# A hybrid RWKV and conformer layer: the prompt unit's steps, the conv layer norm and the head norms in one mixed sequence, w_out with the prompt tile last, router weights side by side

## What is computed

```python
h = rms_norm(x) * (1 + sc1) + sh1
z = h @ w_in                                # 2816 columns
y_rwkv = bidirectional RWKV-7 scan of z     # 8 heads x 64, chunks of 64 tokens
y_rwkv = layer_norm per head (y_rwkv) * (sigmoid(z_g) @ gate_lora_b)
y_conv = silu(layer_norm over 512 channels (depthwise conv of width 31))
x = x + g1 * (concat(y_rwkv, y_conv) @ w_out)
h = rms_norm(x) * (1 + sc2) + sh2
logits = h @ router_group_w (4 columns), h @ router_expert_w (32 columns)
x = x + g2 * top-2 of 8 experts in the top-1 of 4 groups
outputs: rms_norm(x) of prompt and sample tokens, final states of the prompt scan
```

## Time and profile before

| | us |
|---|---|
| median of 3 runs | 1273.71 |
| the profiled execution's own time | 1268.37 |
| its span in the trace | 1266.5 |
| TensorE busy in the span | 949.6 (75%) |
| VectorE busy | 610.0 (48%) |
| ScalarE busy | 293.9 (23%) |
| GpSimd busy | 63.3 (5%) |

### The profile page before, as it was taken

How to read it: one execution, slowest core, us unless ns; L and a number is a source line. 1 busy time by engine, 2 the same in 40 slices (tenths; PEclk the granted TensorE clock), 3 DMA queues, 4 the chain that set the end, 5 groups by cost and what they waited for, 6 DMA issues and landing times. The chain is left out here.

```text
span 1266.5 us, 15551 instructions
## 1 busy us (share of the span) xinstructions
PE 949.6 (75%) x5991; PEld 598.4 (47%) x5991; DVE 610.0 (48%) x1283; ACT 293.9 (23%) x499; POOL 63.3 (5%) x55
## 2 busy tenths in 40 slices
PE   1699988989488778786867666997359998589654
PEld 1365555666275565774756533554333433134221
DVE  2317999364667678678772342424631111011106
ACT  2240000321615335166021243101001111011002
POOL 0000000000010010010100000000111111010000
PEclk9999997999566575575665867987559999799878
DMA  9845512101100110011005191111189999799633
GB/s 326 301 183 203 210 44 71 60 18 26 17 10 18 18 26 17 2 27 17 10 24 163 49 366 78 50 50 50 57 313 375 420 419 419 319 401 420 278 123 140
DMA packets 72745, 193.77 MB, mean 153 GB/s; under 512 B 42310, under 2 KB 42816, under 8 KB 58464
## 3 DMA queue, kind: packets, MB, share of 16 engines
q1 hardware_dynamic: 64416, 174.19, 36.7%
q0 software_dynamic: 5472, 10.53, 2.3%
q10 hardware_dynamic: 2783, 8.06, 1.7%
HBM read 181.80 MB, written 19.34 MB: 159 GB/s over the span
## 5 line engine op out<-in xcount | busy, mean ns | idle before, releaser
L544 PE MATMUL bank<-arena 128*128 128x320 f32 x704 | 201.3, 446 | 12.2 <-DVE arena L436 3.8
L544 PEld LDWEIGHTS bank<-arena 128*128 128x128 f32 x704 | 136.1, 196 | 79.0 <-issue 28.0
L2031 PE MATMUL bank<-arena 128*64 128x512 f32 (+2 forms) x528 | 130.7, 655 | 33.6 <-DMA arena<-in_expert_w_up 32.6
L944 DVE SCALAR_TENSOR_TENSOR arena<-arena 128x655 f32<-128x655 f32 x116 | 104.7, 902 | 4.6 <-DVE arena L944 0.2
L2031 PEld LDWEIGHTS bank<-arena 128*64 128x64 f32 (+2 forms) x528 | 46.1, 149 | 116.4 <-issue 115.0
L1475 PE MATMUL bank<-arena 128*128 128x512 f32 x160 | 76.9, 643 | 11.6 <-issue 11.6
L2111 DVE TENSOR_TENSOR arena<-arena,bank 128x256 f32<-128x256 f32 x17 | 7.2, 422 | 159.8 <-ACT arena L2085 159.8
L2053 PE MATMUL bank<-arena 128*64 128x512 f32 (+2 forms) x264 | 62.4, 599 | 9.9 <-DVE arena L2114 9.9
L906 ACT ACTIVATE arena<-bank 64x128 f32<-64x128 f32 (+1 forms) x68 | 19.9, 292 | 174.3 <-PE bank L1279 173.0
L1475 PEld LDWEIGHTS bank<-arena 128*128 128x128 f32 x160 | 32.8, 208 | 53.0 <-issue 53.0
L1270 PE MATMUL bank<-arena 64*64 64x64 f32 x320 | 25.6, 302 | 40.9 <-DVE arena L1129 33.2
(11 more groups left out here) (321 smaller groups left out, 1445.8 us busy)
## 6 DMA issues: line engine op xcount, KB each, us to landing
arena<-in_expert_w_gate SPq DMA_DIRECT2D x33, 1024.0 KB, 17.0
arena<-in_expert_w_up SPq DMA_DIRECT2D x33, 1024.0 KB, 20.4
arena<-in_expert_w_down SPq DMA_DIRECT2D x33, 1024.0 KB, 18.8
arena<-in_ada_w SPq DMA_DIRECT2D x12, 2048.0 KB, 10.6
arena<-in_w_in SPq DMA_DIRECT2D x22, 512.0 KB, 3.7
arena<-expert_rows SPq DMA_DIRECT2D x10, 512.0 KB, 7.3
arena<-in_x_sample SPq DMA_DIRECT2D x8, 512.0 KB, 7.5
arena<-in_w_out SPq DMA_DIRECT2D x1, 4096.0 KB, 15.9
```

Source lines behind the costliest of these rows:

```text
L544: mm = nc.tensor.matmul(psum[4 + 2 * (n % 2) + half][:, 0:HALF], wring[:, n % NWIN, k], hT[:, k, half * HALF:(half + 1) * HALF], start=(k ...
L944: chain(nc.vector.scalar_tensor_tensor(acc, src, w, acc, ALU.mult, ALU.add))
L2031: mm = nc.tensor.matmul(psum[2 + n % 2][r, :], xeT[:, n % 2, c, r], gu[:, :, c, :], start=(c == 0), stop=(c == KD - 1))
```

## The change

The chain events of unit 4 leave the lists of `order()` and are called one by one from `pe_out`, `dve_out` and `act_out`, with work of the stage behind between them. The convolution's loads move into SyncE's `final`, behind the load of `w_out` and waits for the reads of the PSUM banks of unit 4. The head norms are split into sample tokens (one piece of 512 columns for each pair) and prompt tokens (all four pairs as one piece of 512 columns). The squares and deviations have buffers of their own. w_out takes the tiles 1, 2, 3, 4, 0. The two router matrices are loaded side by side into one array of 36 columns. The sums of the tiles are announced in halves. GpSimd's clearing waits for the last turned tile instead of the logits. In the cut diff the places left out are, in order: two rows of `g1b`; `sh2b`, `gain2` and `norm2_g`; the eight stores of the states; then `late`, the router's weights and biases, `g2b` and the two fixed experts; on TensorE the 8 products each for conv's sums and squares, and behind the gates the prompt heads' mean and four gates of 128 columns, whose variance comes after the first half of tile 1; on VectorE conv's centring (8 instructions), its variance, and at the end conv's scaling (4), the four sample pairs' scaling and gating (8), then the prompt's; on ScalarE four squares of conv, and at the end Ln of four pairs, Exp of conv and of four pairs, four Silu, and the prompt's square, Ln and Exp.

```diff
@@ order() @@
-                       for u in range(NU) for i in range(steps(u)) for ev in CHAIN]
+                       for u in range(NU - 1) for i in range(steps(u)) for ev in CHAIN]
@@ sp_mix(), event final @@
                     sp.dma_start(wout, ins["w_out"][0].rearrange("(k p) n -> p k n", p=P)).then_inc(s_wout, 16)
-                    sp.wait_ge(s_finc, 1)
-                    for a in range(8):
-                        sp.dma_start(outs["new_state"][0, 0, a // 4, 2 * (a % 4):2 * (a % 4) + 2]
...
+                    for use in ("z0", "z1", "y0", "y1", "b0", "b1", "v0", "v1", "v2", "v3", "m0", "m1", "m2", "m3"):
+                        wait_read(sp, u, use)
+                    for stored in s_cst:
+                        sp.wait_ge(stored, 32)
+                    for j in range(4):
+                        sp.dma_start(conv[:, j], cout[j]).then_inc(s_conv_in, 16)
@@ sp_out() @@
+            sp.wait_ge(s_gvar, 5)
+            for i in (1, 2, 3, 0):
+                sp.dma_start(x2[:, i], tok_src(i)).then_inc(s_x2in, 16)
             sp.wait_ge(s_Y, step_at(NU - 1, 2))
...
+            sp.wait_ge(s_cn, 4)
+            sp.dma_start(x2[:, 4], tok_src(4)).then_inc(s_x2in, 16)
...
+            sp.wait_ge(s_finc, 1)
...
+            sp.wait_ge(s_finst, 128)
+            sp.wait_ge(s_mixa, PAIRS)
...
@@ pe_out() @@
+            pe_mix([("X", LAST, 0)])
+            y_mean(0)
+            y_mean(1)
+            pe_mix([("T", LAST, 0)])
...
             pe.wait_ge(s_conv_in, 64)
...
+            pe_mix([("S", LAST, 0), ("Y", LAST, 0)])
+            pe.wait_ge(s_gsq, 4)
...
+            pe_mix([("X", LAST, 1)])
+            y_var(0)
+            y_var(1)
+            pe_mix([("T", LAST, 1)])
+            y_mean(2)
+            y_mean(3)
+            pe_mix([("S", LAST, 1), ("Y", LAST, 1)])
+            y_gate(0)
+            y_gate(1)
+            y_var(2)
+            y_var(3)
+            pe_mix([("final", LAST, 0)])
+            y_gate(2)
+            y_gate(3)
...
             pe.wait_ge(s_mixa, 4)
             pe.wait_ge(s_mixc, 4)
             pe.wait_ge(s_wout, 16)
...
+                for k in range(KD):
+                    mm = nc.tensor.matmul(psum[6][:, 36 * i:36 * i + 36], h2T[:, k], rw_[:, k],
+                                          start=(k == 0), stop=(k == KD - 1))
...
+            for q, i in enumerate(WTILES):
                 if i == 0:
+                    pe.wait_ge(s_mixa, 5)
...
@@ dve_out() @@
+            dve_mix(chain, [("X", LAST, 0)])
+            y_centre(0, 1)
+            y_centre(1, 2)
+            dve_mix(chain, [("T", LAST, 0)])
...
+            dve_mix(chain, [("S", LAST, 0), ("Y", LAST, 0)])
...
+            dve_mix(chain, [("X", LAST, 1)])
+            y_variance(0)
+            y_variance(1)
+            dve_mix(chain, [("T", LAST, 1)])
+            y_centre(2, 4)
+            y_centre(3, 5)
+            dve_mix(chain, [("S", LAST, 1), ("Y", LAST, 1)])
+            y_variance(2)
+            y_variance(3)
...
@@ act_out() @@
+            act_mix(chain, [("T", LAST, 0)])
...
             square(0)
+            square(1)
+            act_mix(chain, [("T", LAST, 1)])
+            square(2)
+            square(3)
+            act_mix(chain, [("final", LAST, 0)])
+            act.wait_ge(s_gv, 1)
+            chain(nc.scalar.activation(rstd, rstd, ACT.Ln))
...
@@ pool_route() @@
-            pool.wait_ge(s_wo, TILES)
-            pool.wait_ge(s_lg, TILES)
+            pool.wait_ge(s_wo, 2 * TILES)
+            pool.wait_ge(s_h2t, TILES)
```

More of the change, by code:

```diff
@@ L740, in sp_mix @@
             sp = nc.sync
-            for ev, u, i in order("sp"):
+            for ev, u, i in order("sp") + [("final", NU - 1, 0)]:
                 if ev == "w":
@@ L923, in gc @@
                 return x.rearrange("p (g c) -> p g c", c=C)
-            chain(nc.vector.memset(VP[:, 0:C], 0.0))
-            chain.announce(nc.vector.memset(E1[:, :, 0:1], 1.0), s_pads, 1)
-            for ev, u, i in order("dve"):
+            for ev, u, i in events:
                 if ev == "z":
@@ L1158, in pool_mix, with pe_mix @@
                                                            ALU.mult), s_bkh, u + 1)
-        def pe_mix():
+        def pe_mix(events):
             pe = nc.tensor
-            for ev, u, i in order("pe"):
+            for ev, u, i in events:
                 if ev in ("z", "ada", "join"):
@@ L1335, in build @@
         xtmp, xsq, sq_pos = regs.take(D), regs.take(D), regs.take(D)
[L1336 removed]
+        rw_, rb = regs.take(KD, 36), regs.take(36)
         h2T = view(zbase + 3 * PAIRS * ZT + ZT, KD, P)
[L1338 removed]
+        routing = Region(ebuf[NB - 1], ebuf[NB - 1] + ROUTING)
         h2d = dram("tokens_for_experts", [T, D])
@@ L1432, in pe_out @@
+            for use in ("z0", "z1"):
+                wait_read(pe, LAST, use)
             pe.wait_ge(s_conv_in, 64)
@@ L1532, in dve_out @@
             for j in range(4):
                 chain.announce(nc.vector.tensor_tensor(conv[:, j], conv[:, j], rstd, ALU.mult), s_cn, j + 1)
-            dve.wait_ge(s_modb, 16 * 8)
-            for c in range(2):
-                chain(nc.vector.scalar_tensor_tensor(gain2[:, c], gain2[:, c], 1.0, h2, ALU.add, ALU.mult))
-            dve.wait_ge(s_x2in, 16 * TILES)
-            def taken(i):
-                dve.wait_ge(s_h2t, i + 1)
+            for j in range(PAIRS):
+                y = ysum[:, j, TP:T]
+                g, b_ = PAR["gng"] + j, PAR["gnb"] + j
+                dve.wait_ge(s_gstd, j + 2)
+                chain(nc.vector.scalar_tensor_tensor(y, y, par[:, g:g + 1], rstd_y[:, j], ALU.mult, ALU.mult))
+                dve.wait_ge(s_gate, j + 1)
+                chain.announce(nc.vector.scalar_tensor_tensor(y, y, par[:, b_:b_ + 1], psum[j % 2][:, :],
+                                                              ALU.add, ALU.mult), s_mixa, j + 1)
@@ new lines, in dve_out @@
+            dve.wait_ge(s_gstd, 6)
+            for j in range(PAIRS):
+                g = PAR["gng"] + j
+                chain(nc.vector.scalar_tensor_tensor(yp[:, j], yp[:, j], par[:, g:g + 1], rstd_p[:, j],
+                                                     ALU.mult, ALU.mult))
+            dve.wait_ge(s_gate, 5)
+            for j in range(PAIRS):
+                b_ = PAR["gnb"] + j
+                ins_ = nc.vector.scalar_tensor_tensor(yp[:, j], yp[:, j], par[:, b_:b_ + 1],
+                                                      psum[7][:, j * P:(j + 1) * P], ALU.add, ALU.mult)
+                if j < PAIRS - 1:
+                    chain(ins_)
@@ L1543, in taken @@
+            chain.announce(ins_, s_mixa, 5)
+            dve.wait_ge(s_x2in, 16 * (TILES + 2))
+            def taken(q):
+                dve.wait_ge(s_h2t, q + 1)
                 chain.announce(nc.vector.tensor_copy(h2T[:, 4:8], psum[5][:, :].rearrange("p (k t) -> p k t", t=P)),
-                             s_h2Td, i + 1)
-            for i in range(TILES):
+                             s_h2Td, q + 1)
+            for q, i in enumerate(WTILES):
                 c = int(i > 0)
-                dve.wait_ge(s_wo, i + 1)
@@ L2200, in _ @@
             chain = act_front()
-            act_mix(chain)
+            act_mix(chain, order("act"))
             act_out(chain)
@@ L2211, in _ @@
             chain = dve_front()
-            dve_mix(chain)
+            dve_pads(chain)
+            dve_mix(chain, order("dve"))
             dve_out(chain)
@@ L2230, in _ @@
             pe_front()
-            pe_mix()
+            pe_mix(order("pe"))
             pe_out()
```

302 lines of the change are left out of this document (149 added, 153 removed).

## The result

The changed kernel takes 1224.13 us (median of 4 runs, 1220.1 to 1225.81), the kernel before 1273.75 (4 runs beside them): a ratio of 0.961, 95% interval 0.9584 to 0.9636. That is 49.6 us less; forecast were 40.6. The profiled execution took 1223.6 with a span of 1221.9, so against the span before (1266.5) the traces account for 44.6 us. As far as these traces show, much of the spread between executions lies ahead of the change: in the eleven profiles with the change (its first, its repeat and nine with one or two edits), the prompt unit's chain starts between 687.5 and 694.0. So the stages are compared by their lengths, each from a first instruction to the next stage's first: the zeroed state on VectorE (L1107 before, L1110 after), the first w_out product, the first routing instruction (128x180), the end.

The account below looks back on a forecast made before the run. No engine bounds the kernel throughout; 88 us ahead of w_out are handing over between engines. Parts A -26.0, B -11.6 and C -3.0 sum to -40.6 us: 1233.1 against the median 1273.7, range 1224 to 1254.

Parts of the forecast that it names:

- Part A: Merged stage ahead of w_out: norm and conv work laid into the prompt chain's gaps, w_out starting about 750.5, -26.0 us.
- the wait: TensorE ahead of w_out's first turn, waiting for h2 and its positions: stall of 0 to 5.5 us, taken as +1.5.
- the chain as it was: 27.2 us: First term of part A: the prompt unit's chain along TensorE, from 688.3 to 715.5, at its old duration.
- the walk: Part A's count along TensorE, then ScalarE and VectorE, to w_out: -26.0 us; -32.5 at full clock, -7.5 at 1.2 GHz.
- The conv loads and the fixed experts' loads: Moved loads: conv's land at 694, wanted at 698; the fixed experts' go out near 764, used after routing; both covered.
- Part B: w_out: variance +0.9, logits -6.3 and -3.5, last tile -4.2, first turn's stall +1.5, together -11.6 us.
- The rule on turn-taking: Positions' DMA beside the fixed experts' loads: engines alternate queues by packet, so landing about 6 us, stall 1.
- Part C: GpSimd's clearing ends before the logits, so VectorE's second routing instruction takes about 0.2 instead of 3.22 us: -3.0.
- 1 (half clock throughout): Merged stage: clock stays at 1.2 GHz, part A only -7.5, in all -22, 1251.6 us; chance 0.15.
- 2 (late positions): First w_out turn: positions land after 10.6 us, TensorE stalls 5.5, in all -36.6, 1237.1 us; chance 0.12.
- 3, 4 and 5: Table switches cost 2.6 us more (0.03); conv loads 26 us late, 1259.1 (0.02); w_out at 1.2 GHz, 1299.4 (0.03).
- three signs of being wrong: PEclk 0.50 from 697 to 735, TensorE idle before the first turn waiting for h2, or a longer expert stage.

Follow-up runs that it names:

- experiment 6: The changed kernel with Ln and Exp alternating again for conv and the four sample pairs, ten table loads instead of two: 1234.59 us.
- experiments 4 and 8: The changed kernel with the first positions' DMA issued earlier: 1218.22 us; with SyncE issuing the fixed experts' loads only after those positions landed: 1217.16 us.
- experiment 3: The changed kernel with GpSimd's clearing of the gather buffers behind the last logits again: 1227.32 us.
- experiment 5: The changed kernel with w_out's tiles in the order 0, 1, 2, 3, 4 again, the prompt first: 1232.8 us.
- experiment 7: The changed kernel with five products of 512 columns that nobody reads put on TensorE ahead of the first turn: 1223.81 us.

## Why the prediction was right, point by point

- **Direction and range**: held, the range by luck: the median is 1224.13 with the end at 1224, and two of the four runs (1223.6 and 1220.1) lie below it. Each mechanism of parts A to C was seen; two sizes were off, part A's by 6 us and the wait's by 5.5.
- **Part A, -26.0; measured -32.0.** The term that was mis-sized is the first, "the chain as it was: 27.2 us". I priced what was added at its clock, and left the chain's own products at their durations of before. In the trace the copies of the end states begin at 725.1 and end at 726.3, 38.8 us after the chain's start, not 43.1 behind it. T is 1.3 shorter and the first S and Y take 3.2 us where they took 5.0; over both steps the chain's own products are together some 5 us shorter. The transposes of the end states take 1.04, at full clock, where I had added 1, and the gates and variances ahead of them 3.5 instead of 4.5. The squares, on the other side, were late by 2.14, which I had counted as nothing. With the events put back ahead of the norms (experiment 1) T is at 3.67 again. From the copies to w_out 17.4 us (19.0 in the walk). That is close to my lower bound, the walk at full clock (-32.5).
- **The table loads**: 1.28 each and no more, shown by experiment 6.
- **The conv loads and the fixed experts' loads**: the first were covered, as said. The second were covered as to their own use, but not as to what they hold up. They went out at 752.6 to 755.7, just ahead of the positions at 756.4.
- **Part B, -11.6; measured -10.1, near by errors of opposite sign.** Laid side by side, the rows of the two kernels give: the four logits blocks on the path -10.1 at equal clock, against -9.8; the tiles behind them -2.0, which I had at nothing; the first two tiles -1.8, since w_out now starts at full clock; the variance +0.9 and the tail -4.1, as counted (the last turn waits 5.52 us behind VectorE, with no positions); the wait +4.4, and turn and logits at half clock behind it +2.6, where I had +1.5 for both. Experiment 2, which puts the 32 records back, finds more for the logits, 13.8 to 15.6; experiments 4 and 8 find 7.0 to 8.8 for the wait. The wait's mechanism was named, with its bound (landing after 10.6, a stall of 5.5); the value I chose between the ends was the wrong one, with 8.8 measured where I took 6.5. The positions were issued 1.3 us earlier than I had them and TensorE wanted h2 2.0 earlier. And the price of the wait left out that the clock falls in it.
- **The rule on turn-taking** (the Trainium skill, DMA: Bandwidth & Descriptors, Queues, rings and completion order) had given, as an estimate, about 6 us for the landing; the trace shows 8.8, between it and the gathers' 10.6. The trace agrees that the transfer does not wait behind all 6 MB: it landed at 765.2, while the last of the six loads, issued before it at 755.7, took 19.2 us.
- **Part C, -3.0**: 3.22 to 0.18 in the row; in the stage 2.2 us against the first profile of the change and 3.7 against the repeat (experiment 3). My argument that a PSUM operand isn't held rested on a row whose instruction started 0.05 us before the clearing; it came to no test.
- **Rivals**: 1 (half clock throughout) is refuted by 1.00 in 697 to 715.6; 2 (late positions) came true in mechanism and price (4.4 for the wait alone, 5.5 forecast), hidden in the total by the larger gains; 3, 4 and 5 did not happen. TensorE idle in front of the first turn was one of the three signs of being wrong, and it was seen; the first w_out record at 743.7 was just ahead of the 744 to 757 named as right; the rest (370.5 and 369.0 against 372 less 3) and the table loads came as said.
- **Total**: against the profiled execution's own time I forecast 1227.8 and it was 1223.6. The remaining 5 us between 44.6 and 49.6 fit the profiled execution of before, a short one (5.4 below its median); where in the span it was short no trace shows.

What stays open: how the 19.6 us of the regrouping divide. Experiment 6 puts the table loads at 6.5 to 8.1 us in the new order, and experiment 5 the prompt's heads ahead of w_out at 8.9 to 10.5. Each was taken back alone, never both together; that they add up to the 19.6 is not shown, and fewer hand-overs, the moved loads and split columns were only argued. Open too is why one tile in four behind a full-clock logits block takes 15.68 us and not 13.98.

## What to carry to other kernels

Work laid into the gaps of a latency-bound chain can pay twice: here the gaps were used, and TensorE's clock stayed up for the chain's own products as well (1.00 against 0.80). Price the whole stretch at the clock it will have, not only the additions. When a bulk load moves, ask what small transfer it now meets: a half-MB load with 6 MB beside it took 8.8 us instead of 3.7, and one wait or an earlier issue gave back more than most of the planned terms. Short products whose records cost the same whatever their columns are worth merging, here for more than their own time (11.7 us in the blocks, 13.8 to 15.6 in the stage). And repeat the profile of the unchanged version before you give a microsecond of a stage to a cause.

## What was not expected of the hardware

- A wait of 4.39 us on TensorE cost 7.0 to 8.8: by the rows the wait itself, turn 1.97 instead of 1.04 and logits 3.60 instead of 1.95. Filling the wait with products that nobody reads (experiment 7) gave 2.0 us back in turn and logits and took 1.1 in the next tile.
- In the profiles with the change, TensorE's tiles of 32 records take 13.98 or 15.68 us with no idle time in them and the same 1.95 us of logits ahead (18 and 6 of 24), and in all profiles 15.25 to 16.45 behind logits of 32 records (six of six), with a granted clock of 0.85 to 0.91 where they are long. The changed kernel and its repeat differ in this in the same tile.
